# Order of the expert units: the first light one is the third, two pairs of heavy ones stand in the middle, and the first gate is made piece by piece

## The chip, the cores and the metric

One core of one Trainium2 chip runs the whole program. The time is the device time of one launch in microseconds; the median of three runs of the kernel before is 1301.4 us (1299.74 to 1305.11).

## The reference, cut to what matters

Two layers of a decoder trunk over 256 tokens of width 1024. The first layer ends in a dense SwiGLU, the second in a mixture of eight experts, of which each token uses two:

```python
def moe_swiglu(x, w_router, we_gate, we_up, we_down):      # D_FF_EXPERT = 3584
    logits = (x @ w_router).astype(jnp.float32)
    top_vals, top_idx = lax.top_k(logits, TOP_K)            # TOP_K = 2
    gates = jax.nn.softmax(top_vals, axis=-1)
    ...
    for e in range(N_EXPERTS):                              # 8
        out = out + combine[..., e:e + 1] * swiglu(x, we_gate[e], we_up[e], we_down[e])
```

All weights are float32: 3 x 1024 x 3584 numbers for each expert, 352 MB for the eight. The products are made from two rounded parts of each number (high and low), as high x high, high x low and low x high.

## The kernel before

After the router, the kernel gathers each expert's tokens and works expert by expert, each in four quarters of its 3584 columns. A quarter is a **unit**; there are 32. Four experts are **heavy** (up to 128 tokens; three matmuls for each product) and the four with the fewest tokens are **light** (up to 64 tokens, high and low part side by side in one operand; two matmuls for each product, and a fold of the two halves afterwards). `ORDER` (L80) is the order of the units by kind: `HHH`, twelve times `LH`, `H`, `LLLL`. Expert 0 is the first heavy one; which expert is any other is known only after the router, and SyncE reads that from `expert_of` before it issues the first load of a light unit (L526 to L529).

**Pieces.** The weights of a unit come as 12 pieces: 4 of the gate and 4 of the up projection (128 x 1792 numbers, 0.92 MB each), and of the down projection 3 of 1.05 MB and one of 0.52 MB, 11.0 MB in all. A piece passes five stations: SyncE loads it into one of 6 slots of `raw` (`load`, L443; it waits until the piece six places ahead has been split); ScalarE rounds it into one of 4 slots of `w_hi` (L656; it waits until TensorE has used the piece four places ahead); VectorE makes `w_lo` (`split_lo`, L1018); TensorE multiplies. A unit i multiplies 4 gate pieces, and then its up pieces mixed with the down pieces of unit i-1 as `ududduud` (`mixed`, L120). Between the first and second gate piece TensorE transposes the h of unit i-1 (`turn_h`, L2026), for which VectorE must have made it (`times_up`, L1385).

**Order on the engines.** ScalarE and VectorE go through the pieces in the same order, with other work at fixed places of unit i (loops at L904 and L1526): after the last piece of the unit comes the work on fetched tokens (`round_tokens` on ScalarE, `rest_of_tokens` on VectorE), then two pieces of the next unit, then `times_up`, `after_up` (routing tables in units 0 to 3) and the next two pieces.

**Tokens of an expert.** For all experts but 0 the tokens are fetched: TensorE sums the indices (`sum_tokens`, L2147, in the units of `SUM_AT`), VectorE copies them (`know_tokens`), GpSimd issues an indirect DMA into `more_rows` (`fetch_tokens`), TensorE transposes the rows (`turn_tokens`, L2156, in the units of `VISITS`), ScalarE and VectorE split them, and TensorE waits for both before the next unit's gate (`before_gate`). For the first light expert the sum is made in the middle of unit 1 and the transposition in the middle of unit 2, ahead of its third up piece (`amid_up`, L2188).

**The first gate** (`first_gate`, L2198) makes high x high for all 4 pieces, then high x low for all, then low x high for all, and gives up each piece in the last round.

Of the kernel before, what the change touches and what calls it, by code (L numbers as in the profile page):

```python
# [14 lines left out]
def hybrid_trunk_kernel(nc, x_in, w_in, conv_w, v_g, v_b, w_s, b_s, out_g, w_out, ln1_g, ln1_b, ln2_g, ln2_b,  # L15
# [11 lines left out]
    NT = TOK // P  # L27
# [51 lines left out]

    ORDER = "HHH" + "LH" * 12 + "H" + "L" * QUARTERS  # L80
    assert ORDER.count("H") == HEAVIES * QUARTERS and ORDER.count("L") == LIGHTS * QUARTERS

# [19 lines left out]
    FETCHED = (("L", 0), ("H", 1), ("L", 1), ("H", 2), ("L", 2), ("H", 3), LAST_ONE)  # L102
    VISITS = ((2, 0), (3, 1), (8, 2), (10, 3), (13, 4), (16, 5), (20, 6))
    KEPT = sorted([ek for ek in FETCHED if ek != LAST_ONE] + [("H", 0)], key=lambda ek: units(*ek)[-1])
    SUM_AT = (1, 4, 5, 6)
    PICK_AT = 7
# [46 lines left out]
    with ctx:  # L153
# [168 lines left out]
        gateT_bank, upT_bank = turn[:, 2, 0:PART], turn[:, 3, 0:PART]  # L322
        sums_bank = turn[:, 1, PART:PART + 4]
        tokens_bank = turn[:, 0:2, :].rearrange("p b c -> p (b c)")
# [117 lines left out]
        def _(sp):  # L442
# [81 lines left out]
            for which, i, pair in IN_ORDER:  # L524
                k, s = expert_step(i)
                if (which, i, pair) == ("gate", ORDER.index("L"), 0):  # L526
                    sp.wait_ge(tokens_known, 1)
                    ranked_expert = [sp.value_load(expert_of[0:1, q:q + 1], min_val=1, max_val=E - 1)
                                     for q in range(OTHERS)]  # L529
# [475 lines left out]
        def _(dve):  # L1005
# [413 lines left out]
            def rank_experts():  # L1419
# [16 lines left out]
                step(nc.vector.tensor_reduce(slot_at, ranked, X, ALU.add))  # L1436
                choose(0)
                step(nc.vector.tensor_tensor(below, at_rank, slot_iota[:, 1:E].unsqueeze(1).to_broadcast(
                    [P, OTHERS, OTHERS]), ALU.mult))
                step(nc.vector.tensor_reduce(expert_at, below, X, ALU.add))  # L1440
                nc.vector.tensor_copy(expert_of, expert_at)

# [52 lines left out]
            def know_tokens(j):  # L1495
                n = len(FETCHED[2 * j:2 * j + 2])
                dve.wait_ge(tokens_summed, j + 1)
                nc.vector.tensor_copy(token_of[:, 2 * j:2 * j + n],
                                      sums_bank[:, 0:2 * n:2]).then_inc(tokens_known, 1)

# [25 lines left out]
            for i in range(N_UNITS):  # L1526
# [7 lines left out]
                else:  # L1534
                    if i:
                        rest_of_h(i - 1)
                    splits(b, b + 1)
                split_lo(b + 2)
                if kept_at(i) is not None and KEPT[kept_at(i)][0] == "L":
                    fold_ys(kept_at(i))  # L1540
# [4 lines left out]
                splits(b + 3, min(unit_end, ahead))  # L1545
                if i in SUM_AT:
                    know_tokens(SUM_AT.index(i))
# [116 lines left out]
        def _(pe):  # L1664
# [482 lines left out]
            def sum_tokens(j):  # L2147

                pe.wait_ge(pick_ready, NT + j + 1)
                for c in range(len(FETCHED[2 * j:2 * j + 2])):  # L2150
                    for n in range(NT):
                        last = nc.tensor.matmul(sums_bank[:, 2 * c:2 * c + 2], pick[:, n, c, :],
                                                token_ids[:, n, :], start=(n == 0), stop=(n == NT - 1))
                last.then_inc(tokens_summed, 1)
# [24 lines left out]
            def before_gate(i):  # L2179

                if visit_at(i - 1) is not None:
                    pe.wait_ge(xg_done, visit_at(i - 1) + 1)
                if i - 1 in SUM_AT:
                    pe.wait_ge(tokens_known, SUM_AT.index(i - 1) + 1)
# [3 lines left out]
            def amid_up(i):  # L2188

                gate_left(i)  # L2190
                if i in SUM_AT:
                    sum_tokens(SUM_AT.index(i))
                if visit_at(i) is not None:
                    turn_tokens(visit_at(i))
# [3 lines left out]
            def first_gate():  # L2198

                w = [wide_rows([a[:, (MOE_AT + pair) % PARTS, :] for a in (w_hi, w_lo)]) for pair in range(4)]  # L2200
                for k in range(KD):
# [4 lines left out]
                    for c in range(2):  # L2206
                        nc.tensor.matmul(gate_banks[:, c, :], xg_hi[0][:, k, :], w[k // 2][0][:, k % 2, c, :],
                                         start=(k == 0), stop=False)
                for k in range(KD):
                    if k % 2 == 0:  # L2210
                        pe.wait_ge(*split_of(MOE_AT + k // 2))
                    for c in range(2):
                        nc.tensor.matmul(gate_banks[:, c, :], xg_hi[0][:, k, :], w[k // 2][1][:, k % 2, c, :],
                                         start=False, stop=False)
                for k in range(KD):
                    if k % 4 == 0:
                        pe.wait_ge(xg_lo_ready, k // 4 + 1)
                    for c in range(2):
                        last = nc.tensor.matmul(gate_banks[:, c, :], xg_lo[0][:, k, :], w[k // 2][0][:, k % 2, c, :],
                                                start=False, stop=(k == KD - 1))  # L2220
                    if k % 2:
                        last.then_inc(piece_used, 1)

# [26 lines left out]
            for i in range(N_UNITS):  # L2250
                if i == 0:
                    first_gate()
                else:
                    before_gate(i)
                    for pair in range(4):
                        if pair == 1:
                            turn_h(i - 1)
                        rows_pair(i, 0, pair)
                    turned_left(i - 1)
                pairs = {"u": 0, "d": 0}  # L2260
                for c in mixed(i):
# [4 lines left out]
                    else:  # L2266
                        if pairs[c] == 2 and i == N_UNITS - 1:
                            turn_h(i)
                        down(i - 1, pairs[c])
                    pairs[c] += 1  # L2270
# [57 lines left out]
```

## Time and profile before

| | before |
|---|---|
| median of 3 runs | 1301.4 us |
| the profiled execution | 1302.68 us, its span 1300.9 us |
| busy share of the span: TensorE, VectorE, ScalarE | 96%, 85%, 72% |
| granted TensorE clock, mean over the span | 0.993 |
| mean over the span of what the DMAs moved | 334 GB/s |

The expert stage runs from 374 us (first gate) to 1286 us (last down product). Its units follow each other on TensorE, and a stretch from the end of one to the end of the next can be read from the busy times by window. A line of such a view gives the stretch, its length, the busy time and instruction count of TensorE (PE), its weight loads (PEld), VectorE (DVE), ScalarE (ACT) and GpSimd (POOL), then the granted clock, the share of time that the DMA engines were busy, and the rate in GB/s. TensorE's idle time is the length less its busy time.

### The profile page before, as it was taken

To read this page: it belongs to the slowest core of one execution; us is meant where nothing else is said; L and a number is where in the kernel's file an instruction comes from. 1 tells how busy PE (TensorE), PEld (TensorE's weight loads), DVE (VectorE), ACT (ScalarE), POOL (GpSimd) and SP (SyncE) were. 2 spreads that over 40 slices of the span, in tenths; PEclk is the share of its full clock that TensorE was granted. 3 is DMA by queue.
4 is the path that set the end of the run, shared out by engine and by line. 5 is a ranking of instruction groups with operands and counts; after the bars stand their busy time and mean duration, and the time that the engine had idled before them with its cause. 6 is when DMAs were issued, how large, how long until landed. Compare 5 with 4: busy or idle time off the path is not lost.

```text
span 1300.9 us, 16398 instructions
## 1 busy us (share of the span) xinstructions
PE 1247.5 (96%) x6471; PEld 1087.2 (84%) x6471; DVE 1105.6 (85%) x871; ACT 930.2 (72%) x720; POOL 43.3 (3%) x57
## 2 busy tenths in 40 slices
PE   9999999999999999999999999999999999999884
PEld 8988888888888888888897888889888898988673
DVE  6977555577979899898989999899998989999895
ACT  5575444454867787788878788788887878888772
POOL 1100000001010000000000000000000000000010
PEclk9999999999999999999999999999999999999997
DMA  9947555536559999999999999999999999999991
GB/s 325 345 141 273 187 189 193 194 135 218 167 186 363 344 412 358 409 410 406 398 405 396 402 410 411 403 396 398 413 394 411 400 402 412 400 406 397 410 410 37
DMA packets 143558, 434.52 MB, mean 334 GB/s; under 512 B 8964, under 2 KB 50996, under 8 KB 131188
## 3 DMA queue, kind: packets, MB, share of 16 engines
q1 hardware_dynamic: 139936, 421.07, 84.6%
q0 software_dynamic: 3456, 12.32, 2.7%
q8 instruction: 53, 0.87, 0.3%
q14 instruction: 29, 0.24, 0.1%
q10 hardware_dynamic: 84, 0.02, 0.0%
HBM read 428.40 MB, written 4.98 MB: 333 GB/s over the span
## 4 chain that ended last, share of the span: by engine, by line
PE 70%; DVE 17%; DMA 6%; ACT 4%; issue 3%; POOL 0%; SPq 0%; ACTq 0%; DVEq 0%; POOLq 0%
DVE w_lo L1016 14%; PE turn L1679 7%; PE turn L1681 7%; PE turn L1680 7%; PE accp L1679 6%; PE accp L1681 6%; PE accp L1680 6%; PE turn L1791 4%; PE turn L1788 4%; ACT w_hi L656 3%; PE turn L2022 3%; DMA raw<-in_we_gate 3%; PE accp L2049 3%; PE accp L2051 3%; DMA raw<-in_we_up 2%
## 5 line engine op out<-in xcount | busy, mean ns | idle before, releaser
L1016 DVE TENSOR_TENSOR w_lo<-raw,w_hi 128x2048 fp32r<-128x2048 f32 (+3 forms) x449 | 900.4, 2041 | 113.5 <-ACT w_hi L656 110.7
L656 ACT CAST w_hi<-raw 128x1792 fp32r<-128x1792 f32 (+2 forms) x443 | 755.4, 1725 | 185.2 <-PE turn L1681 48.7
L2099 PE MATMUL turn<-w_hi,t_both 128*128 128x448 f32 x512 | 192.1, 375 | 20.5 <-DVE w_lo L1016 18.8
L2100 PE MATMUL turn<-w_lo,t_both 128*128 128x448 f32 x512 | 187.3, 366 | 0.0
L1679 PE MATMUL turn<-w_hi,a_hi 128*128 128x448 f32 x496 | 184.2, 371 | 2.9 <-DVE w_lo L1016 2.8
L1680 PE MATMUL turn<-w_lo,a_hi 128*128 128x448 f32 x496 | 181.8, 366 | 0.0
L1681 PE MATMUL turn<-w_hi,a_lo 128*128 128x448 f32 x496 | 181.7, 366 | 0.0
L2099 PEld LDWEIGHTS turn<-w_hi,t_both 128*128 128x128 f32 x512 | 96.1, 188 | 40.3 <-issue 18.4
L1679 PEld LDWEIGHTS turn<-w_hi,a_hi 128*128 128x128 f32 x496 | 93.2, 188 | 14.0 <-DVE w_lo L1016 3.7
L2100 PEld LDWEIGHTS turn<-w_lo,t_both 128*128 128x128 f32 x512 | 96.4, 188 | 7.9
L1680 PEld LDWEIGHTS turn<-w_lo,a_hi 128*128 128x128 f32 x496 | 93.2, 188 | 8.4
L1681 PEld LDWEIGHTS turn<-w_hi,a_lo 128*128 128x128 f32 x496 | 93.2, 188 | 8.1
L1679 PE MATMUL accp<-w_hi,hT_hi 128*128 128x512 f32 x224 | 89.0, 397 | 5.7 <-DVE w_lo L1016 5.7
L1788 PE MATMUL turn<-t_both,w_hi 128*128 128x512 f32 x232 | 91.8, 396 | 0.0
L1791 PE MATMUL turn<-t_both,w_hi 128*128 128x512 f32 x232 | 91.8, 396 | 0.0
L1681 PE MATMUL accp<-w_hi,hT_lo 128*128 128x512 f32 x224 | 87.5, 391 | 0.0
L1680 PE MATMUL accp<-w_lo,hT_hi 128*128 128x512 f32 x224 | 87.4, 390 | 0.0
L2049 PE MATMUL accp<-w_hi,hT_hi 128*128 128x512 f32 x210 | 83.8, 399 | 3.2 <-DVE w_lo L1016 1.9
L2051 PE MATMUL accp<-w_lo,hT_hi 128*128 128x512 f32 x210 | 82.8, 394 | 0.0
L1790 PE MATMUL turn<-t_both,w_lo 128*128 128x256 f32 x232 | 64.6, 278 | 0.0
L1789 PE MATMUL turn<-t_both,w_lo 128*128 128x256 f32 x232 | 64.3, 277 | 0.0
L1679 PE MATMUL accp<-w_hi,a_hi 128*128 128x512 f32 x152 | 59.5, 391 | 0.0
(291 smaller groups left out, 1562.0 us busy)
## 6 DMA issues: line engine op xcount, KB each, us to landing
raw<-in_we_gate SPq DMA_DIRECT2D x128, 896.0 KB, 7.6
raw<-in_we_up SPq DMA_DIRECT2D x128, 896.0 KB, 9.4
raw<-in_we_down SPq DMA_DIRECT2D x96, 1024.0 KB, 10.0
raw<-in_w_in SPq DMA_DIRECT2D x18, 1024.0 KB, 8.9
raw<-in_we_down SPq DMA_DIRECT2D x32, 512.0 KB, 7.7
raw<-in_w_down SPq DMA_DIRECT2D x11, 1024.0 KB, 5.0
raw<-in_w_gate SPq DMA_DIRECT2D x10, 1024.0 KB, 5.2
raw<-in_w_up SPq DMA_DIRECT2D x10, 1024.0 KB, 5.2
```

What stands on the lines that cost most here:

```text
L656: nc.scalar.copy(w_hi[:, p % PARTS, 0:filled(p)], raw[:, p % RING, 0:filled(p)]).then_inc(hi_done, 1)
L1016: return nc.vector.tensor_tensor(out, whole, hi.bitcast(f32), ALU.subtract)
L1679: nc.tensor.matmul(to, lh, rh, start=start, stop=False, **group)
L1680: nc.tensor.matmul(to, lh, rl, start=False, stop=False, **group)
L1681: return nc.tensor.matmul(to, ll, rh, start=False, stop=stop, **group)
L1788: nc.tensor.matmul(whole, wh[:, k, at], xT_pair[:, k, :], start=(k == 0), stop=False)
L1790: nc.tensor.matmul(first, wl[:, k + 1, at], xT_hi[:, k + 1, :], start=False, stop=False)
L1791: last = nc.tensor.matmul(whole, wh[:, k + 1, at], xT_pair[:, k + 1, :], start=False, stop=(k == KD - 2))
L2049: nc.tensor.matmul(accp[:, 2 + c, :], hT_packed[:, block, :], wh[:, j, cols], start=(first and block == 0), stop=False)
L2051: last = nc.tensor.matmul(accp[:, 2 + c, :], hT_packed[:, block, :], wl[:, j, cols], start=False, stop=(last_one and block == BLOCKS - 1))
L2099: nc.tensor.matmul(to[:, c, :], few, wh[:, kk, c, :], start=(k == 0), stop=False)
L2100: last = nc.tensor.matmul(to[:, c, :], few, wl[:, kk, c, :], start=False, stop=(k == KD - 1))
```

## The change

`ORDER` gets its first light unit at place 2 (counted from 0) in place of 3, one heavy unit stands beside another at places 9 and 10 and at 18 and 19, and only one stands ahead of the last four light units. `VISITS` and `SUM_AT` follow. The first light expert's indices are summed right after the gate of unit 1, its tokens are transposed ahead of the last down piece of unit 1 (after all up pieces), SyncE waits for the table of experts alone, and `first_gate` finishes one piece after the other.

```diff
-    ORDER = "HHH" + "LH" * 12 + "H" + "L" * QUARTERS
+    ORDER = "HH" + "LHLHLHLHH" * 2 + "LHLHLHLH" + "L" * QUARTERS
...
-    VISITS = ((2, 0), (3, 1), (8, 2), (10, 3), (13, 4), (16, 5), (20, 6))
+    VISITS = ((1, 0), (4, 1), (8, 2), (10, 3), (13, 4), (16, 5), (21, 6))
...
-    SUM_AT = (1, 4, 5, 6)
+    SUM_AT = (1, 3, 5, 6)
...
-        sums_bank = turn[:, 1, PART:PART + 4]
+        first_sums, later_sums = accp[:, 2, 0:4], turn[:, 1, PART:PART + 4]
...
-                    sp.wait_ge(tokens_known, 1)
+                    sp.wait_ge(pick_ready, NT + 1)
...
-                choose(0)
                 step(nc.vector.tensor_tensor(below, at_rank, slot_iota[:, 1:E].unsqueeze(1).to_broadcast(
                     [P, OTHERS, OTHERS]), ALU.mult))
                 step(nc.vector.tensor_reduce(expert_at, below, X, ALU.add))
-                nc.vector.tensor_copy(expert_of, expert_at)
+                step(nc.vector.tensor_copy(expert_of, expert_at))
+                choose(0)
...
                 split_lo(b + 2)
+                if i == SUM_AT[0]:
+                    know_tokens(0)
...
-                if i in SUM_AT:
+                if i in SUM_AT[1:]:
                     know_tokens(SUM_AT.index(i))
...
-                if visit_at(i) is not None:
+                if visit_at(i):
                     turn_tokens(visit_at(i))
...
-                for k in range(KD):
-                    if k % 2 == 0:
-                        pe.wait_ge(*split_of(MOE_AT + k // 2))
-                    for c in range(2):
-                        nc.tensor.matmul(gate_banks[:, c, :], xg_hi[0][:, k, :], w[k // 2][1][:, k % 2, c, :],
-                                         start=False, stop=False)
-                for k in range(KD):
-                    if k % 4 == 0:
-                        pe.wait_ge(xg_lo_ready, k // 4 + 1)
-                    for c in range(2):
-                        last = nc.tensor.matmul(gate_banks[:, c, :], xg_lo[0][:, k, :], w[k // 2][0][:, k % 2, c, :],
-                                                start=False, stop=(k == KD - 1))
-                    if k % 2:
-                        last.then_inc(piece_used, 1)
+                for pair in range(4):
+                    pe.wait_ge(*split_of(MOE_AT + pair))
+                    pe.wait_ge(xg_lo_ready, pair // 2 + 1)
+                    for k in (2 * pair, 2 * pair + 1):
+                        for c in range(2):
+                            nc.tensor.matmul(gate_banks[:, c, :], xg_hi[0][:, k, :], w[pair][1][:, k % 2, c, :],
+                                             start=False, stop=False)
+                            last = nc.tensor.matmul(gate_banks[:, c, :], xg_lo[0][:, k, :], w[pair][0][:, k % 2, c, :],
+                                                    start=False, stop=(k == KD - 1))
+                    last.then_inc(piece_used, 1)
...
+                    if i == SUM_AT[0]:
+                        sum_tokens(0)
                     turned_left(i - 1)
...
+                        if pairs[c] == 3 and visit_at(i) == 0:
+                            turn_tokens(0)
                         down(i - 1, pairs[c])
```

## Rows read from the trace of the kernel before

**Rows 1.** The page, its parts 1 and 2: TensorE over the span; GB/s in 40 slices

```profile
PE 1247.5 (96%) x6471; PEld 1087.2 (84%) x6471; DVE 1105.6 (85%) x871; ACT 930.2 (72%) x720; POOL 43.3 (3%) x57
GB/s 325 345 141 273 187 189 193 194 135 218 167 186 363 344 412 358 409 410 406 398 405 396 402 410 411 403 396 398 413 394 411 400 402 412 400 406 397 410 410 37
```

**Rows 2.** Busy times by window: later units 22 (H), 23 (L), 27 (H after H)

```profile
988.53:1017.87 29.34, 29.34 (x154) 26.56 (x153) 25.43 (x15) 23.12 (x17) 0.58 (x1) 1.00 1.01 399
1017.87:1043.22 25.35, 24.09 (x114) 20.50 (x114) 24.73 (x15) 21.73 (x16) 0.00 (x0) 1.00 1.02 412
1127.25:1157.09 29.84, 29.84 (x146) 26.73 (x146) 27.14 (x17) 23.24 (x16) 0.55 (x1) 1.00 1.02 413
```

**Rows 3.** The same view of two light units with longer waits, 11 and 19

```profile
683.53:710.39 26.86, 24.44 (x114) 20.42 (x114) 26.03 (x16) 22.55 (x16) 0.59 (x1) 1.00 1.02 394
906.82:933.01 26.19, 24.35 (x115) 20.42 (x114) 25.59 (x16) 22.18 (x16) 0.59 (x1) 1.00 1.02 413
```

**Rows 4.** The same view of the last light units 28, 30 and 31

```profile
1157.09:1181.94 24.85, 23.87 (x115) 20.58 (x114) 24.17 (x15) 21.21 (x16) 0.00 (x0) 1.00 0.99 383
1207.72:1237.79 30.07, 24.88 (x120) 19.77 (x120) 25.06 (x15) 22.59 (x17) 0.00 (x0) 1.00 1.02 410
1237.79:1271.84 34.05, 29.46 (x148) 24.18 (x148) 32.65 (x20) 25.51 (x19) 3.50 (x2) 0.95 0.92 371
```

**Rows 5.** The same view, units 0 to 6, from TensorE's end of one to the next

```profile
374.20:395.83 21.63, 20.14 (x99) 18.19 (x99) 18.34 (x20) 13.75 (x10) 0.00 (x0) 1.00 0.70 248
395.83:426.61 30.78, 30.59 (x150) 27.11 (x150) 28.03 (x31) 22.32 (x15) 0.97 (x1) 1.00 0.98 371
426.61:458.58 31.97, 31.09 (x154) 27.08 (x154) 29.10 (x42) 23.09 (x17) 0.98 (x1) 1.00 0.96 348
458.58:485.19 26.61, 25.09 (x121) 20.91 (x120) 25.25 (x20) 21.46 (x16) 0.00 (x0) 1.00 1.02 410
485.19:515.46 30.27, 30.05 (x158) 27.27 (x158) 26.93 (x22) 22.91 (x17) 2.45 (x1) 1.00 0.97 365
515.46:542.13 26.67, 25.21 (x118) 20.36 (x116) 24.90 (x19) 20.56 (x14) 0.00 (x0) 1.00 1.02 395
542.13:572.14 30.01, 29.80 (x156) 27.05 (x156) 26.96 (x19) 24.42 (x19) 0.58 (x1) 1.00 1.02 410
```

**Rows 6.** Chain of waits, first gate and token transposition: start, length, engine, tile, line

```profile
374.38 3.35 PE turn L2207 x16
377.73 3.31 PE turn L2213 x16
381.04 0.84 PE turn L2219 x4
381.96 1.70 ACT w_hi L656
...
451.49 0.64 PE turn L2161 x8
```

**Rows 7.** Timeline of GpSimd: the fetch of the first light expert's tokens

```profile
420.71 0.97 POOL L617 DMA_INDIRECT more_rows<-token_rows,numbers  x1 [50.82 <-DVE numbers L1498]
```

**Rows 8.** Timeline of ScalarE and VectorE, between units 1 and 2 and between 2 and 3

```profile
419.99 1.69 ACT L656 CAST w_hi<-raw 128x1792 fp32r<-128x1792 f32 x1 [1.67 <-PE accp L1681]
...
452.17 0.59 ACT L887 CAST t_both<-turn 128x512 fp32r<-128x512 f32 x1 [2.25 <-PE turn L2161]
...
426.55 1.08 DVE L1388 TENSOR_TENSOR h_e<-turn,y_work 128x896 f32<-128x896 f32 x1
...
431.09 3.96 DVE L1016 TENSOR_TENSOR w_lo<-raw,w_hi 128x1792 fp32r<-128x1792 f32 x2 [0.26 <-DVE ranking L1475]
434.97 1.08 DVE L1016 TENSOR_TENSOR hT_lo<-turn,hT_hi 128x896 fp32r<-128x896 f32 x1
435.97 15.56 DVE L1016 TENSOR_TENSOR w_lo<-raw,w_hi 128x1792 fp32r<-128x1792 f32 x8
```

**Rows 9.** Busy times by window: three light up pieces

```profile
461.03:466.25 5.22, 5.18 (x24) 4.01 (x23) 5.22 (x4) 5.18 (x4) 0.00 (x0) 1.00 1.02 414
```

More of the change, by code:

```diff
@@ L1498, in know_tokens @@
                 nc.vector.tensor_copy(token_of[:, 2 * j:2 * j + n],
-                                      sums_bank[:, 0:2 * n:2]).then_inc(tokens_known, 1)
+                                      (later_sums if j else first_sums)[:, 0:2 * n:2]).then_inc(tokens_known, 1)
             def add_rows(j):
@@ L2151, in sum_tokens @@
                     for n in range(NT):
-                        last = nc.tensor.matmul(sums_bank[:, 2 * c:2 * c + 2], pick[:, n, c, :],
+                        last = nc.tensor.matmul((later_sums if j else first_sums)[:, 2 * c:2 * c + 2], pick[:, n, c, :],
                                                 token_ids[:, n, :], start=(n == 0), stop=(n == NT - 1))
@@ L2182, in before_gate @@
                     pe.wait_ge(xg_done, visit_at(i - 1) + 1)
-                if i - 1 in SUM_AT:
+                if i - 1 in SUM_AT[1:]:
                     pe.wait_ge(tokens_known, SUM_AT.index(i - 1) + 1)
@@ L2190, in amid_up @@
                 gate_left(i)
-                if i in SUM_AT:
+                if i in SUM_AT[1:]:
                     sum_tokens(SUM_AT.index(i))
-                if visit_at(i) is not None:
+                if visit_at(i):
                     turn_tokens(visit_at(i))
```

## Prediction, written before the changed kernel ran

> **What bounds the kernel now.** I read the page first: TensorE is busy 96% of the span, and from the 15th slice on the DMAs move about 400 GB/s [rows 1]. Two resources are near their limit, so the averages don't decide. Next I cut the expert stage at the ends of its units on TensorE. Three paces come out: a heavy unit after a light one takes 29.34 us without a hole, a heavy one after a heavy one 29.84, a light one after a heavy one 25.35 with 1.26 idle [rows 2]. The light unit's hole is VectorE's: it makes 12 pieces and two passes on h in a unit in which TensorE needs only 24.1 us. The transfers need 11.01 MB at the 412 GB/s of the best windows = 26.7 us a unit, 53.4 a pair against 54.7. So in the middle TensorE, with VectorE's hole once a pair, sets the pace, and the transfers are 1.3 us a pair faster; where GpSimd's transfers take part of the DMA time, the hole in the light unit grows (2.42 and 1.84 us; four such units, 11, 15, 17 and 19, by 2.4 us in all over 1.26) [rows 3]. The last four light units are bound by the transfers: unit 30 takes 30.07 us, of which TensorE works 24.88 [rows 4]. The early units are above the pace: unit 1 30.78 (pace 29.84), unit 2 31.97 (29.84), unit 3 26.61 (25.35), unit 4 30.27 (29.34), unit 5 26.67 (25.35), unit 6 30.01 (29.34) [rows 2, 5]. That is what a change of order can win: the sum of the pace over the 32 units is the same for both orders, since each has three heavy units behind a heavy one and twelve light ones behind a heavy one.
>
> **The change, part by part.** I count TensorE's idle and extra time up to the end of the last heavy unit, and then pass it to the end.
>
> First gate. Before, piece 0 is given up after 36 matmuls; the chain shows 16 in 3.35, 16 in 3.31, 4 in 0.84, then ScalarE's cast of the fifth piece at 381.96 [rows 6]. After, it takes 16 + 8 matmuls: 374.4 + 3.35 + 1.67 = 379.4, so the cast and VectorE's split come 2.4 us earlier. TensorE itself ends the 48 products at the same 384.3, and only its wait of 1.49 us (21.63 - 20.14) goes [rows 5]: **-1.5**. Nothing else is late next: the fifth piece is then split by 383.5.
>
> Tables and SyncE. `choose(0)` comes about 0.7 us later on VectorE; its reader is now the sum after the gate of unit 1, some 5 us later: 0. SyncE reads the experts' numbers ahead of piece 0 of unit 2, which is not wanted on ScalarE until about 424: 0. The first fetch is issued earlier: `know_tokens(0)` moves ahead of five splits (about 409 in place of 420). In the trace GpSimd issued it at 420.71 [rows 7], 31 us before its transposition, so its landing time can't be read as a need; the transposition is now at about 423.7, 14 us after the issue. A piece of 0.92 MB at 412 GB/s takes 2.2 us; I take it as landed, and if the fetch were slower than 14 us all that follows moves by the difference.
>
> The transposition for unit 2. This is the costly part. Before, it stands ahead of two up pieces and a down piece, about 6.4 us of TensorE's work; ScalarE stood 2.25 us waiting for it at 452.17 [rows 8] and TensorE felt nothing. After, it stands behind both up pieces, with one down piece of 6 matmuls (1.4 us) as cover, while ScalarE and VectorE still have to pass it before they may touch the gate pieces of unit 2. Queued behind ScalarE's wait are all four casts of that gate, queued behind VectorE's are the four splits, `times_up(1)` and the routing tables. With unit 1 about 1.5 us early: last up piece done 423.7; transposed 424.4 (0.64 [rows 6]); down piece done 425.8; ScalarE tokens 425.0 (0.59), cast 426.7 (1.70); VectorE split 428.7 (1.98, half of 3.96 [rows 8]). TensorE stands from 425.8 to 428.7: hole 2.9. A light pair of pieces is 8 matmuls, 1.65 (24 in 5.18 [rows 9]; the same for gate). Second split 430.7, h product (1.08) 431.7: hole 1.3 before the transposition of h, which ends 432.6. Before, VectorE needed from 427.6 to 431.1 for the tables and another 3.96 for two splits [rows 8]; after, 431.7 to 435.2, splits at 437.2 and 439.1. TensorE had finished the second piece at 434.3: hole 2.9; third piece 438.8: hole 0.3; then h's low part and the first up piece (442.1): hole 1.3, and 0.6 at the first down piece. VectorE goes on without a gap as it did at 435.97 (8 in 15.56 us), ends its unit near 455.5 against 451.5, and TensorE is full again. Holes 9.3 in place of the paced 1.26: **+8.0**; the token transposition now counts in unit 1: +0.7; unit 2's own excess before goes (31.97 - 29.84): **-2.1**. From the two sides: 0 if pieces already split cover the wait, 9.3 if nothing does; the dependence of each station on the one before leaves at most the 1.4 us of the down piece as cover, so I take 8.0.
>
> Units 3 to 6. Heavy unit 3 has the sum of indices and a late start (0.8 over pace, before 1.3): -0.5. Light unit 4 enters with TensorE full, but VectorE's choice and weights fall between its second and third gate piece, and it carries a heavy token transposition: +2.4 over pace against 0.9: +1.5. Units 5 and 6: 0.5 and 0.4 against 1.3 and 0.7: **-1.1** [rows 5].
>
> Sum to here: -1.5 + 8.0 + 0.7 - 2.1 - 0.5 + 1.5 - 1.1 = **+5.0**.
>
> The middle. A TensorE that runs 5 us later no longer feels the extra holes of the four light units: **-2.4** [rows 3]. The two pairs of heavy units cost 29.84 in place of 29.34 each, as the pairs that go did: 0. So the last heavy unit ends 2.6 later.
>
> The last four light units go by the transfers. Before, the lag of a pair of heavies at their head slows these (383 in place of 412 GB/s in 24.85 us = 1.7 us of transfer time [rows 4]); with one heavy there, this goes: -1.7. The write of light expert 2's rows (0.26 MB, 0.6 us) moves into this stretch: +0.6. In all **+1.5 us**: the profiled execution's 1302.68 becomes 1304.2. It is 1.3 above the median, so I predict 1302.9, say 1303 for the median.
>
> The holes near 428 and 436 are 2.9 us each; the longest that a row of an early unit can hold is 1.49, and the granted clock stays at 1.00 in all of them [rows 5], while it is 0.95 in 1237.79 to 1271.84, with 4.59 us idle [rows 4]. The Trainium skill (TensorE: Matmul & The Clock Gate, Part 1) has an idle TensorE fall back to half its clock. By that rule one such fall would cost what the last row shows, 5% of 34 us = 1.7, and the sum would be +3.2; by the rows of the early units it is 0.
>
> **The rivals.** (A) *The early stretch was the loss and goes.* If splits made ahead cover the wait, unit 2 keeps its pace: the +1.5 above becomes 1.5 - 8.0 = -6.5, 1296.2 for the profiled execution and 1295 for the median. For it: transfers in units 1 and 2 run at 371 and 348 GB/s. Against it: ScalarE already waited 2.25 us with far more cover. The Trainium skill (Perfetto Trace Analysis, Optimization Strategy) advises interleaving regimes whose most-contended engine differs, which is this case.
>
> (B) *The transfers are the true line from unit 5 on.* Then the hole of 8 us is won back, and only their own lead counts: the first gate frees pieces 2.4 us earlier, unit 3's heavy work takes it back in part: -1, 1300.4. For it: 410 GB/s in units 3 and 6 [rows 5]. Against: the 1.3 us a pair.
>
> (C) *The pairs of heavy units in the middle stop the transfers.* At units 9/10 and 18/19 TensorE enters 5 us late; each heavy pair puts it 2 x 29.6 - 2 x 26.7 = 5.8 us further behind. From the point where its lag is more than the four split pieces and the filled slots hold, a load waits, and units 11 and 20 then wait for data. I price each at 3.1 (29.84 - 26.7): +1.5 + 2 x 3.1 = +7.7, 1309. For it: transfers lost 1.7 behind the old pair. Against: one such pair at pace ran with 413 GB/s [rows 2].
>
> **Chances.** Forecast 0.46 (1299 to 1307), A 0.17, B 0.18, C 0.17, others 0.02. One measurement of this kernel tells no less than about 0.5%, 6.5 us, from no change; so faster by over 0.5% is 0.16 (most of A), within it 0.65 (forecast, B, the rest), slower 0.19 (C and a hole larger than 9.3). The range that should hold 8 of 10 takes in the ends of A and C: 1294.5 to 1310.5.
>
> **What would show it.** Right: TensorE idle some 9 us between 425 and 445; ScalarE waiting over 6 us for the token transposition between units 1 and 2; VectorE idle as long; the fifth piece's cast near 379.5; two heavies in a row at 29.8; the last heavy unit ending near 1160 (before 1157.1). Wrong: a unit 2 of 26 us (A), a last heavy ending at or before 1156 (B), units 11 or 20 longer than 27 us with waits on DMA (C), or a fetch that lands after 423.7.

## The result, and the profile after the change

| | before | after |
|---|---|---|
| median | 1300.91 us, 20 runs (1298.43 to 1305.11) | 1304.2 us, 20 runs (1302.78 to 1307.81) |
| ratio to before, 95% interval | 1 | 1.0028, 1.002 to 1.0035 |
| profiled execution, its span | 1302.68, 1300.9 us | 1306.46, 1304.7 us |
| last heavy unit ends on TensorE | 1157.09 | 1159.84 |
| first three quarters of the last down product's columns end ("end") | 1285.71 | 1289.39 |

In every kernel here the last quarter of those columns ends 3.33 to 3.34 us after "end" (1289.05 before, 1292.73 after), so differences of "end" are differences of the last product too.

The change costs 3.6 us by the ratio (1300.91 x 0.0028); the two medians are 3.3 apart. The forecast was 1303.0, with a sum of +1.5 where the ratio shows +3.6 and the two profiled executions +3.8. Both lie inside 0.5%.

The share of time in which TensorE is busy is 96%, as before [rows 1]. Of the GB/s in the expert stage the 12th to 16th slices differ most (208, 338, 336, 387, 380 for 186, 363, 344, 412, 358). The page after, parts 1 and 2:

```profile
span 1304.7 us, 16401 instructions
...
GB/s 320 343 145 268 188 192 192 193 135 216 171 208 338 336 387 380 399 409 398 406 407 391 388 411 411 403 386 404 411 397 400 403 400 399 413 398 412 410 413 41
```

Cut at the ends of the units, as in [rows 5] (stretch, length, then busy time and count of PE, PEld, DVE, ACT, POOL, the granted clock, DMA share, GB/s). Units 0 to 6 after the change:

```profile
374.87:394.91 20.04, 20.04 (x99) 18.23 (x99) 18.69 (x20) 14.00 (x10) 0.00 (x0) 1.00 0.81 291
394.91:426.33 31.42, 31.42 (x158) 27.27 (x156) 24.44 (x29) 19.28 (x14) 3.56 (x2) 1.00 0.91 337
426.33:459.14 32.81, 27.35 (x114) 22.36 (x115) 31.11 (x41) 25.90 (x19) 0.18 (x1) 0.90 0.92 337
459.14:488.94 29.80, 29.80 (x158) 27.00 (x157) 26.02 (x20) 22.20 (x16) 0.00 (x0) 1.00 1.00 384
488.94:516.86 27.92, 25.48 (x122) 20.84 (x120) 26.56 (x25) 22.09 (x16) 0.91 (x1) 1.00 1.00 389
516.86:547.16 30.30, 30.08 (x158) 27.28 (x158) 26.25 (x17) 23.03 (x17) 0.00 (x0) 1.00 1.02 380
547.16:573.11 25.95, 24.49 (x116) 20.65 (x116) 25.32 (x18) 21.85 (x16) 0.00 (x0) 1.00 1.02 412
```

The first gate has no idle time any more (20.04 of 20.04). Unit 2, a light one with 24.1 us of work at pace [rows 2], takes 32.81 us: TensorE idles 5.46, and its own 114 matmuls take 27.35 because the granted clock is 0.90. How it comes to stand there is on ScalarE, VectorE and GpSimd, the counterparts of [rows 7, 8] (start, length, engine, line, operation; in brackets the idle time before it and its releaser):

```profile
380.13 3.36 ACT L656 CAST w_hi<-raw 128x1792 fp32r<-128x1792 f32 x2 [2.11 <-PE turn L2218]
...
424.80 0.59 ACT L887 CAST t_both<-turn 128x512 fp32r<-128x512 f32 x1 [7.11 <-PE turn L2163]
```

```profile
425.42 0.69 DVE L1016 TENSOR_TENSOR t_both<-turn,t_both 128x512 fp32r<-128x512 f32 x1 [6.45 <-ACT t_both L887]
427.00 3.96 DVE L1016 TENSOR_TENSOR w_lo<-raw,w_hi 128x1792 fp32r<-128x1792 f32 x2 [0.90 <-ACT w_hi L656]
430.88 1.08 DVE L1388 TENSOR_TENSOR h_e<-turn,y_work 128x896 f32<-128x896 f32 x1
431.88 0.87 DVE L1125 TENSOR_SCALAR pick<-slot_iota,ranking 128x128 fp32r<-128x128 f32 x4
...
435.19 3.96 DVE L1016 TENSOR_TENSOR w_lo<-raw,w_hi 128x1792 fp32r<-128x1792 f32 x2
```

```profile
409.84 2.76 POOL L617 DMA_INDIRECT more_rows<-token_rows,numbers  x1 [39.30 <-DVE numbers L1498]
```

ScalarE stands 7.11 us until the transposition, VectorE 6.45; then VectorE does two splits, the h product, 3.3 us of routing tables (431.88 to 435.19) and only then the next two splits. TensorE waits for each of them. Its waits in unit 2 (line, what it waited for: us in total, times, longest):

```profile
PE turn L2101 <- DVE w_lo L1016: 4.5, 3, 2.8
PE turn L2017 <- DVE h_e L1388: 0.6, 1, 0.6
PE accp L1681 <- DVE w_lo L1016: 0.3, 1, 0.3
```

The clock, which the forecast held at 1.00, falls. The windows around the first hole:

```profile
426.30:429.20 2.90, 0.05 (x2) 0.06 (x1) 2.20 (x2) 2.90 (x3) 0.21 (x1) 1.00 1.01 416
429.20:431.00 1.80, 1.80 (x8) 1.48 (x8) 1.80 (x2) 1.80 (x2) 0.00 (x0) 0.86 1.02 327
431.00:433.00 2.00, 1.38 (x7) 0.98 (x6) 2.00 (x11) 0.73 (x1) 0.00 (x0) 0.50 1.02 400
433.00:435.00 2.00, 2.00 (x8) 1.87 (x7) 1.73 (x15) 1.17 (x2) 0.00 (x0) 0.50 1.04 355
435.00:437.00 2.00, 1.78 (x5) 1.03 (x4) 1.97 (x2) 1.45 (x2) 0.00 (x0) 0.50 0.47 197
437.00:439.00 2.00, 1.73 (x8) 1.44 (x8) 2.00 (x2) 1.78 (x1) 0.00 (x0) 0.92 0.38 66
```

TensorE works 0.05 us in a stretch of 2.90; behind it the clock is 0.86 and then 0.50 (1.2 of 2.4 GHz), and it is back within 437 to 439. In the same place the transfers fall to 66 GB/s: the slots are full, and SyncE waits up to 5.9 us for a split before it may load again (between 430 and 442).

The heavy pair in the middle (units 9, 10, 11), the last heavy unit and the last light ones:

```profile
628.82:658.16 29.34, 29.34 (x154) 26.56 (x153) 25.80 (x15) 22.46 (x16) 0.00 (x0) 1.00 1.02 402
658.16:688.88 30.72, 30.72 (x154) 27.57 (x154) 27.85 (x17) 24.06 (x17) 1.51 (x2) 1.00 1.03 408
688.88:714.11 25.23, 23.95 (x114) 20.50 (x114) 24.54 (x15) 21.48 (x16) 0.00 (x0) 1.00 1.00 388
1130.50:1159.84 29.34, 29.34 (x153) 26.55 (x153) 26.28 (x15) 23.25 (x17) 0.00 (x0) 1.00 1.02 395
1159.84:1186.05 26.21, 24.38 (x115) 20.42 (x114) 25.76 (x16) 22.98 (x17) 0.55 (x1) 1.00 1.02 414
1186.05:1211.84 25.79, 24.11 (x121) 19.74 (x119) 23.49 (x14) 21.09 (x16) 4.95 (x3) 1.00 1.02 412
1211.84:1241.78 29.94, 24.86 (x121) 19.77 (x120) 25.13 (x15) 22.64 (x17) 0.00 (x0) 1.00 1.02 410
1241.78:1275.65 33.87, 29.34 (x149) 24.34 (x148) 32.63 (x20) 25.54 (x19) 3.49 (x2) 0.95 0.93 377
```

Heavy units in a row lose nothing: 30.72 with no idle time, 0.9 over the 29.84 of [rows 2] with 8 more matmuls (the transposition of tokens), and the light unit behind keeps 25.23. Unit 28, the first of the last four, takes 26.21 where it took 24.85 [rows 4].

### The profile page after: what moved, and what is told of

Its sections match the earlier page's. It is cut to its first block, busy times and chain, and to the rows that moved or that the text cites. A ratio compares the mean times of both kernels' runs of the same rounds, so it can differ in the third digit from the quotient of the medians.

```text
span 1304.7 us, 16401 instructions
## 1 busy us (share of the span) xinstructions
PE 1249.5 (96%) x6471; PEld 1089.2 (83%) x6471; DVE 1104.5 (85%) x871; ACT 931.5 (71%) x720; POOL 43.1 (3%) x57
## 4 chain that ended last, share of the span: by engine, by line
PE 74%; DVE 16%; DMA 4%; ACT 3%; issue 2%; SPq 0%; ACTq 0%; DVEq 0%
DVE w_lo L1016 12%; PE turn L1681 8%; PE turn L1683 8%; PE turn L1682 8%; PE accp L1681 6%; PE accp L1682 6%; PE accp L1683 6%; PE turn L1793 4%; PE turn L1790 4%; PE turn L2024 3%; ACT w_hi L656 3%; PE accp L2051 3%; PE accp L2053 3%; PE turn L2101 2%; PE turn L2102 2%
```

## The experiments

Every kernel was timed beside the kernel before on the same chip. "Unit 2", "u27" and "end" are of the profiled execution: the length of unit 2 on TensorE, the end of the last heavy unit, and the row of that name in the table above.

**a1: the first gate alone.** The new `first_gate` in the kernel before.

```diff
+ for pair in range(4):
+     pe.wait_ge(*split_of(MOE_AT + pair))
+     ...                       # the three products of this piece, then the piece is given up
- ...                           # before: high x high of all pieces, high x low of all, low x high of all
```

> The kernel before with the new first gate alone. Theory (TensorE's wait of 1.49 us at the first up piece goes, and TensorE sets the pace until the last four units): the cast of the fifth piece comes 2.3 us earlier, the wait is 0, and the end comes up to 1.5 us earlier, 1299.4 to 1300.9 against 1300.9, ratio 0.9988 to 1.0. Rival (the transfers are the line from unit 5 on): the early gain shows in units 0 to 2 and is gone at the end, ratio 1.000.

Measured: 1299.3 us (1296.66 to 1303.36, 11 runs), ratio 0.9988 [0.9978, 0.9998]; u27 1155.62, end 1283.72. The window of unit 0, whose first product begins at 374.76 here:

```profile
374.76:394.80 20.04, 20.04 (x99) 18.23 (x99) 18.69 (x20) 14.01 (x10) 0.00 (x0) 1.00 0.81 288
```

No idle time: 20.04 us in place of 21.63. The last heavy unit ends 1.47 us earlier than in the kernel before. So the 1.6 us of the first gate is gained, and nothing behind gives it back. The changed kernel is some 5.2 us behind this one (0.9988 to 1.0028).

**a2: the transposition earlier.** The changed kernel, with the transposition of the first fetched tokens ahead of the third up piece of unit 1, two up pieces earlier.

```diff
-                if visit_at(i):
+                if visit_at(i) is not None:
                     turn_tokens(visit_at(i))
...
-                        if pairs[c] == 3 and visit_at(i) == 0:
-                            turn_tokens(0)
```

> The changed kernel with one edit: the first light expert's tokens are transposed ahead of the third up piece of unit 1, as all others are, and not ahead of its last down piece. Theory (the late transposition holds ScalarE and VectorE, and so TensorE's unit 2): ScalarE's wait for it falls from 7.1 us to under 3, TensorE's holes in unit 2 from 5.5 us plus 3.3 us of slow matmuls to 3 or less (the tables remain), unit 2 takes 28 to 29 us in place of 32.8, and the end comes 2 to 4 us earlier than the changed kernel, 1300 to 1302, ratio 0.9995 to 1.001. Rival 1 (the fetch has not landed at 419): TensorE waits for it inside unit 1 and nothing is won, ratio 1.003. Rival 2 (the pairs of heavy units cost the 3 us): unit 2 gets short and the end stays, ratio 1.003.

Measured: 1300.05 us (1298.78 to 1300.7, 11 runs), ratio 0.9994 [0.9985, 1.0002]. ScalarE's wait and unit 2:

```profile
419.14 0.59 ACT L887 CAST t_both<-turn 128x512 fp32r<-128x512 f32 x1 [2.25 <-PE turn L2163]
```

```profile
425.56:453.72 28.16, 24.35 (x114) 20.42 (x114) 27.17 (x40) 22.69 (x17) 0.00 (x0) 1.00 0.99 383
```

The wait is the 2.25 us of [rows 8]. The hole ahead of unit 2 is gone and the clock stays at 1.00; unit 2 is 4.65 us shorter, and the time falls by 4.4 us (0.0034 x 1300.9). What is left is 3.8 us of idle time, of which 3.4 are waits for splits behind the tables.

**a3: the tables into the wait.** The changed kernel, late transposition kept; VectorE makes the routing tables of the second half-round (`choose(1)`, `usable_choices()`) while it waits for that transposition, not between two splits of unit 2.

```diff
+                if i == 1:
+                    choose(1)
+                    usable_choices()
                 if visit_at(i) is not None:
                     rest_of_tokens(visit_at(i))
...
-                if i in SUM_AT:
+                if i in SUM_AT[1:]:
                     ...choose
-                if i == 1:
-                    usable_choices()
```

> The changed kernel with one edit: the routing tables that VectorE makes in unit 1 after the h product (3.3 us) stand ahead of its work on the fetched tokens, in the 6.5 us in which it waits for them. Theory: the hole between the second and third gate piece of unit 2 goes, VectorE's unit 2 ends 3.3 us earlier, unit 2 takes about 29.5 us in place of 32.8, and the end comes 2 to 3 us earlier than the changed kernel, 1301 to 1302, ratio 1.000 to 1.0015. Rival (the transfers, not unit 2, set the later part): the end moves by under 1 us, ratio 1.002 to 1.003.

Measured: 1301.38 us (1300.0 to 1302.7, 11 runs), ratio 1.0005 [0.9996, 1.0014]. Unit 2:

```profile
425.84:455.34 29.50, 25.68 (x115) 21.98 (x115) 28.19 (x16) 25.46 (x19) 0.18 (x1) 0.94 1.01 374
```

3.3 us less than in the changed kernel, as many as the tables take; the hole ahead of the unit stays (longest wait 2.9), and with it a fall of the clock to 0.50, for 3.4 us here.

**a4: no fall of the clock.** The changed kernel with 12 unused matmuls of 512 columns behind the last down piece of unit 1, where TensorE has nothing to do. The added products are written where nothing reads them.

```diff
                         down(i - 1, pairs[c])
+                        if pairs[c] == 3 and i == 1:
+                            for _ in range(12):
+                                nc.tensor.matmul(accp[:, 3, :], a_hi[:, 0:P], a_hi[:, 0:BANK], start=True, stop=True)
```

> The changed kernel with 12 idle matmuls of 512 columns (about 2.6 us) added after the last down piece of unit 1; their result is not used. They fill TensorE's hole of 2.85 us, after which the granted clock was 0.50 for some 7 us. Theory: the clock stays at 1.00, but the slow matmuls had lain in waits for VectorE, so unit 2 gets shorter by under 0.7 us and the ratio stays at 1.002 to 1.003. Rival (the fall of the clock is the loss): unit 2 gets shorter by the 3.3 us of extra busy time and the ratio falls to 1.0005 or less.

Measured: 1304.5 us (1303.7 to 1308.41, 6 runs), ratio 1.0036 [1.0024, 1.0049]. The windows of the old hole and of the stretch behind it, and unit 2:

```profile
425.60:428.40 2.80, 2.66 (x13) 1.92 (x11) 2.20 (x2) 2.80 (x3) 0.09 (x1) 1.00 1.02 420
...
432.00:436.00 4.00, 1.94 (x11) 1.47 (x10) 3.69 (x19) 3.65 (x3) 0.00 (x0) 1.00 0.80 296
...
425.51:458.32 32.81, 27.67 (x127) 22.52 (x126) 31.11 (x41) 25.79 (x19) 0.18 (x1) 1.00 0.91 333
```

The clock is full in all of it, and unit 2 takes the same 32.81 us. The slow matmuls of the changed kernel lie in time in which TensorE would wait for VectorE anyway (1.94 us busy of 4.00 here): the fall costs nothing that can be measured.

**b1: one pair into the middle, in the kernel before.** Of the pair ahead of the last four light units, one heavy unit goes to places 10 and 11.

```diff
-    ORDER = "HHH" + "LH" * 12 + "H" + "L" * QUARTERS
+    ORDER = "HHH" + "LHLHLHLHH" + "LH" * 8 + "L" * QUARTERS
```

> The kernel before with one edit: one heavy unit of the pair that stands ahead of the last four light units is moved to the middle (a pair at units 10 and 11, the last heavy unit follows a light one). The start, the first gate and the third unit are untouched. My theory: a pair in the middle costs TensorE nothing (in the changed kernel units 9 to 11 and 18 to 20 kept the pace of 29.3 to 29.8 and 25.2 us), and what the move costs is the stock of landed pieces for the last four light units: at the end of unit 27 the landed data were 11.80 us ahead of TensorE in the kernel before and 8.97 us in the changed one. So the end comes 0.5 to 1.2 us later, ratio 1.0004 to 1.001. Rival C of the prediction, that pairs in the middle stop the transfers: 3 us or more, ratio 1.0025 or over, with idle time of TensorE in units 11 to 14. Third theory, that the order is worth nothing anywhere: ratio 0.9997 to 1.0003 and the same 11.80 us ahead.

**b2: one pair back, in the changed kernel.**

```diff
-    ORDER = "HH" + "LHLHLHLHH" * 2 + "LHLHLHLH" + "L" * QUARTERS
+    ORDER = "HH" + "LHLHLHLHH" + "LH" * 8 + "H" + "L" * QUARTERS
```

> The changed kernel with one edit: the second of its middle pairs is taken out and its extra heavy unit stands ahead of the last four light units, as in the kernel before. First light unit still third, first gate still by pieces, one pair in the middle. My theory: the landed data are again some 11.8 us ahead of TensorE at the end of unit 27, the last four light units take 0.5 to 1.2 us less than in the changed kernel, and the time is 1303.0 to 1303.7 us, ratio to the kernel before 1.0016 to 1.0022 beside 1.0028. If the last stretch is bound by something else than the stock, nothing changes: 1.0028. If the middle pair kept back transfers, it gains more than 1.5 us.

Measured: b1 1300.54 us (1299.37 to 1302.15, 11 runs), ratio 1.0000 [0.9991, 1.0009]; b2 1304.32 us (1303.33 to 1305.97, 8 runs), ratio 1.0029 [1.0019, 1.004], beside 1.0028 without the edit. I had expected a loss of 0.5 to 1.2 us in b1 and a gain of as much in b2, from the stock of landed pieces; neither shows. In the medians the place of a pair is worth nothing within about 1.2 us, either way. In b1 the middle pair and the first of the last four, which now follows a single heavy unit:

```profile
683.32:713.16 29.84, 29.84 (x146) 26.75 (x146) 27.53 (x17) 23.30 (x16) 0.59 (x1) 1.00 1.02 394
...
1155.26:1181.43 26.17, 24.35 (x115) 20.42 (x114) 25.75 (x16) 22.75 (x17) 0.55 (x1) 1.00 1.02 414
```

and the same unit of b2, behind a pair again:

```profile
1159.69:1184.58 24.89, 23.88 (x115) 20.58 (x114) 24.18 (x15) 21.22 (x16) 0.00 (x0) 1.00 0.99 390
```

The pair in the middle runs at 29.84. Unit 28 takes 26.2 without a pair ahead of it and 24.9 with one, in both kernels.

**b3: everything that helps, in the changed kernel**: a2's and a3's edits, and b2's order.

> The changed kernel with three edits: the token transposition stands ahead of the third up piece of unit 1, the routing tables of the second half-round are made by VectorE while it waits for that transposition, and the pair stands ahead of the last four light units. My theory: the hole at the start of unit 2 goes (as when the transposition alone was moved) and the 3.8 us that were left in unit 2 shrink, since VectorE no longer makes the tables between hT_hi and hT_lo: unit 2 takes 26 to 27.5 us, and the end comes at 1297.5 to 1299.5 us, ratio 0.9975 to 0.999. If the transfers are the line by then (rival B's mechanism, the landings of the later units), TensorE's gain in unit 2 comes back as idle time in the light units 8 to 26 and the time is that of the early transposition alone, 1300, ratio 0.9994.

Measured: 1297.15 us (1295.76 to 1299.49, 11 runs), ratio 0.9978 [0.9969, 0.9987], end 1279.95. Unit 2:

```profile
425.98:452.31 26.33, 24.34 (x115) 20.42 (x114) 24.73 (x15) 22.44 (x17) 0.00 (x0) 1.00 1.02 410
```

The light unit in third place keeps nearly its pace (26.33, idle 1.99), 6.5 us less than in the changed kernel; the median is 6.5 us lower as well (0.0050 x 1300.9). What TensorE wins at 452 us arrives at the end.

**b4: the same care for the old order.** The kernel before with the new first gate, and with `usable_choices()` moved into VectorE's wait for the transposition in unit 2.

```diff
-                if i == 1:
-                    usable_choices()
...
+                if i == 2:
+                    usable_choices()
                 if visit_at(i) is not None:
                     rest_of_tokens(visit_at(i))
```

> The kernel before, in its old order of units, with the first gate by pieces and with the routing choices of the second half-round made by VectorE in its wait for the token transposition. My theory: the idle 0.9 us at TensorE in unit 2 goes beside the 1.5 us of the first gate: 1298.3 to 1298.9 us, ratio 0.998 to 0.9985. Rival: the 0.9 us is not set by the choices and the ratio is that of the first gate alone, 0.9988.

Measured: 1296.88 us (1296.33 to 1299.2, 7 runs), ratio 0.9973 [0.9962, 0.9985]. Unit 2, a heavy one here:

```profile
425.09:455.80 30.71, 30.71 (x155) 27.25 (x154) 28.85 (x41) 23.10 (x17) 0.98 (x1) 1.00 0.97 375
```

The 0.88 us of idle time of [rows 5] is gone, and the unit 1.2 us shorter than in a1 (31.93). So the old order, handled with the same care, is as fast as the new one. I had expected 0.998 to 0.9985, and the median is lower than that; of the 2 us below a1 by the ratios, unit 2 explains 1.2.

**c1 and c2: the place of the pairs, with b3's other edits.** c1 has no pair in the middle and three heavy units ahead of the last four light ones; c2 has the changed kernel's order.

```diff
-    ORDER = "HH" + "LHLHLHLHH" + "LH" * 8 + "H" + "L" * QUARTERS     # b3
+    ORDER = "HH" + "LH" * 12 + "HH" + "L" * QUARTERS                 # c1
+    ORDER = "HH" + "LHLHLHLHH" * 2 + "LHLHLHLH" + "L" * QUARTERS     # c2
```

> The kernel of b3 (early transposition, tables in the wait) with no pair in the middle: three heavy units in a row stand ahead of the last four light ones. Stock theory: TensorE falls further behind the landed data in each heavy unit behind another, so at the end of unit 27 they are 12 us or more ahead of it (b3: 10.22; without a pair 9.0 to 9.6), the last stretch takes 126 us or less (b3 126.92, without a pair 128.7 to 129.6), and what this gains is paid back by the middle, which keeps its extra holes in light units: within 1 us of b3, ratio 0.997 to 0.9985. Rival, that the last stretch is set by its transfers alone and the differences between the kernels are scatter: 127 to 129 us whatever stands ahead. Third, that three heavy units stop the transfers: lead 12 us but a landing rate under 390 GB/s in units 25 to 28, end 1 us or more later than b3.

> The kernel of b3 with the pairs where the changed kernel has them, both in the middle and none ahead of the last four light units: early transposition and tables in the wait, together. If the place of the pairs is worth nothing in the median (as b1 and b2 say, 1.0000 and 1.0029 beside 1.0028), the ratio is that of b3, 0.9975 to 0.998, though the last stretch takes 128.7 to 129.6 us in place of 126.9 and the lead at the end of unit 27 is 9.0 to 9.6. If the stock decides, it is 1 us slower than b3: 0.9985 to 0.999.

Measured: c1 1299.32 us (1297.93 to 1301.08, 12 runs), ratio 0.9984 [0.9976, 0.9993]; c2 1298.46 us (1296.6 to 1299.29, 9 runs), ratio 0.9977 [0.9967, 0.9988]. c2 equals b3. In c1 the third heavy unit in a row:

```profile
1125.45:1155.33 29.88, 29.88 (x147) 26.76 (x146) 25.69 (x16) 21.79 (x15) 0.00 (x0) 1.00 1.00 375
```

The transfers fall to 375 GB/s, where the second in a row still had 413 [rows 2]. For these kernels I worked out, from the landing of each piece's last packet, when the pieces of unit 27 had all landed:

```
        landed   TensorE   ahead   end       TensorE to end   pair ahead of the last four
before  1145.30  1157.09   11.80   1285.71   128.62           yes
after   1150.87  1159.84    8.97   1289.39   129.55           no
a1      1144.91  1155.62   10.70   1283.72   128.10           yes
a2      1145.01  1154.02    9.01   1283.24   129.22           no
b1      1146.25  1155.26    9.01   1284.45   129.19           no
b2      1149.25  1159.69   10.44   1286.82   127.13           yes
b3      1142.81  1153.03   10.22   1279.95   126.92           yes
b4      1144.01  1154.38   10.37   1282.20   127.82           yes
c2      1142.19  1151.46    9.27   1279.56   128.10           no
c1      1142.36  1155.33   12.97   1283.24   127.91           three
```

With a pair the last stretch takes 126.9 to 128.6, without one 128.1 to 129.6, and the stock of landed pieces is larger with one. But c1, with the largest stock, isn't shorter still: my stock theory said 126 or less. Its third heavy unit ran with a slower transfer, as the third theory had it. And c2, without the pair, is as fast as b3 in the median. So the stock of landed pieces isn't what sets the end; the difference in the last stretch is largely unit 28's 1.3 us, of which unit 27 gives back 0.5. And most of what c1's "end" lies behind b3's (3.3 us) is there before the last stretch: 2.3 us at the end of unit 27. Where they come from stands in the next section.

## Why the prediction was right, and where its sum was off

The forecast (slightly slower, inside 0.5%) held, and so did the mechanism of its largest term, unit 2. Two terms did not: the middle came out at its number for another reason, and the last four light units went the other way. Its steps, against the profiled executions:

| step | predicted | measured |
|---|---|---|
| first gate | -1.5 | -1.6 in the profiled pair, -1.6 in a1 |
| start of the first gate (no step) | 0 | +0.67 |
| unit 1, the transposition in it | +0.7 | 31.42 - 30.78 = +0.6 |
| unit 2 (holes +8.0, old excess -2.1) | +5.9 | (32.81 - 25.35) - (31.97 - 29.84) = +5.3 |
| unit 3 | -0.5 | (29.80 - 29.34) - (26.61 - 25.35) = -0.8 |
| unit 4 | +1.5 | (27.92 - 25.35) - (30.27 - 29.34) = +1.6 |
| units 5 and 6 | -1.1 | (0.96 + 0.60) - (1.32 + 0.67) = -0.4 |
| middle, to the end of unit 27 | -2.4 | (1159.84 - 1157.09) less the rows above = -2.7 |
| last four light units | -1.1 | 129.55 - 128.62 = +0.9 |
| sum | +1.5 | +3.7 |

**Unit 2, station by station.** The last down piece of unit 1 ended at 426.33 (forecast 425.8), TensorE stood 2.85 us there (2.9); the tables ended at 435.16 (435.2); ScalarE waited 7.11 us (over 6). The fetch landed 7.8 us after its issue at 409.84, well before the 424.1 at which TensorE needed it, so my taking it as landed was right. I had asked for some 9 us of idle time between 425 and 445; there are 5.47, because 3.3 us of what I had down as waiting went into matmuls at half the clock. a2 and a3 show the two parts one at a time: the place of the transposition is worth 4.4 us of the median, the tables between the splits 3.0 (1.0028 to 1.0005).

**The clock.** I held it at 1.00 by rows in which no hole was longer than 1.49 us, and it fell. The Trainium skill's rule (TensorE: Matmul & The Clock Gate, Part 1) had it right that an idle TensorE falls back to half its clock; here it did so behind a hole of 2.85 us. The cost that I attached to the rule, 1.7 us, isn't there: a4 keeps the clock full and gains nothing. My zero for the term was right for another reason than I gave: behind the hole VectorE sets the pace, and TensorE has time to be slow in.

**The step that missed most is "the last four light units go by the transfers": -1.7 and +0.6, measured +0.9.** I read the 383 GB/s of unit 28 [rows 4] as a loss that the heavy pair causes, and so as a gain when the pair goes. Without a pair the rate in unit 28 is 414, as I said, but the unit is longer: 26.21 with 1.83 idle against 24.85 with 0.98. VectorE shows why. In the kernel before it has five splits in a row at this place; in the changed kernel the finished rows of the light expert whose last unit stands two places ahead are added here:

```profile
1162.91 10.56 DVE L1016 TENSOR_TENSOR w_lo<-raw,w_hi 128x1792 fp32r<-128x1792 f32 x5
```

```profile
1166.13 6.15 DVE L1016 TENSOR_TENSOR w_lo<-raw,w_hi 128x1792 fp32r<-128x1792 f32 x3
1172.20 1.21 DVE L1413 TENSOR_TENSOR ys_rows<-accp,ys_rows 64x1024 f32<-64x1024 f32 x1
1173.33 4.47 DVE L1016 TENSOR_TENSOR w_lo<-raw,w_hi 128x2048 fp32r<-128x2048 f32 x2
```

Behind a heavy pair this addition falls into the second heavy unit, where VectorE has time to spare; behind a single one it falls into a light unit, where VectorE is the bound. My ledger gave the light units behind a single heavy one 25.35 everywhere. From unit 28's end to "end" the changed kernel takes 103.34 us and the kernel before 103.77 (1285.71 - 1181.94): 0.4 less, where I gave the transfers 1.1. Over the twelve kernels this stretch takes 101.9 to 103.8 us, so these two single executions don't show that they win anything. Unit 28 alone is +1.36.

**The middle: the right number for the wrong reason.** I let the extra holes of the middle go because TensorE would run 5 us later. In the five kernels with the changed order it reaches the end of unit 6 at 573.11 (after), 572.27 (a4), 569.27 (a3), 567.67 (a2) and 565.85 (c2), and from there to the end of unit 27 it takes 586.73, 585.73, 586.89, 586.35 and 585.61 us: an arrival 7 us earlier brings nothing back. Units 15 and 17, two of the four whose holes were to go, kept them (0.98 us above the pace together before, 1.47 after). What differs is again where the additions fall. There is one for each of the first three light experts. In the kernel before the first stands in light unit 11 and the second in light unit 19, which are the two long ones of [rows 3]; in the changed kernel they stand in the heavy units 10 and 19. The first one, before and after:

```profile
696.23 1.21 DVE L1413 TENSOR_TENSOR ys_rows<-accp,ys_rows 64x1024 f32<-64x1024 f32 x1
```

```profile
670.51 1.21 DVE L1413 TENSOR_TENSOR ys_rows<-accp,ys_rows 64x1024 f32<-64x1024 f32 x1
```

Over all twelve profiled executions, the time of units 7 to 27 above the paces of [rows 2]:

| additions in light units, of units 7 to 27 | kernels | above the paces, us |
|---|---|---|
| two | before, a1, b4, c1 | 8.2 to 8.8 |
| one | b1, b2, b3 | 5.6 to 6.7 |
| none | after, a2, a3, a4, c2 | 4.4 to 5.7 |

Every light unit behind a single heavy one that holds an addition takes 0.8 to 1.7 us over 25.35; what is left in the last row stands in other units and has other causes. So the two pairs in the middle win 2.7 us there, and the missing pair at the end costs 1.4 in unit 28. This also says why b1, b2 and c2 showed nothing: none of them changes how many additions fall in light units in the whole stage (two in before and b1, one in after, b2, b3 and c2); c1 goes from b3's one to two, and its "end" is 3.3 us later, though its median is only 0.8 us behind by the ratios, with overlapping intervals. All this is read from the traces, and no run moved an addition by itself: ScalarE's copy ahead of it (1.0 us) and GpSimd's write of the rows behind it move with it.

Of the 2.2 us between sum and profiled difference, 0.67 is the scatter of single executions: the first gate began that much later (374.09 to 374.87 over the twelve; b2 and a4, with the same code up to there as the changed kernel, at 374.26 and 374.10).

**The rivals.** A, that the early stretch is won, asked for splits made ahead over the wait; the wait was there, and unit 2 took 32.81 and not 26. With the transposition early and the tables in the wait it does take 26.3 to 26.4 (b3, c2): the order would have allowed that part of A, and two placements prevented it. A's price of 1295 is not reached even so (1297.15 in b3). B, that the transfers win the hole back, is refuted: b3 and c2 recover 6.5 us in unit 2 and all of it stays at the end. C, that pairs in the middle stop the transfers, is refuted by b1 and by the windows of units 9 to 11; it takes a third heavy unit in a row (c1, 375 GB/s) before the rate gives way within a heavy unit.

Best measured are b4 (0.9973) and b3 (0.9978), with overlapping intervals: some 3 us below the kernel before. The order itself is worth nothing that their medians can tell; what helped was the first gate by pieces and VectorE's small work put into its waits.

## What to carry to other kernels

When a transposition or another step that two engines must pass moves behind more of TensorE's work, count all that is queued behind it on those engines: it was the largest term here, and going through the stations in order gave its first hole as 2.9 us for the 2.85 measured. Put an engine's small work into a wait that it has anyway, ahead of the waiting instruction and not behind it; that gave 3.0 us in one place and 1.2 us of a unit in another. A window with a lower transfer rate isn't a loss as long as the engine that it feeds doesn't wait: before crediting its end, see what the bound engine of the next unit takes over from the order that goes. Small work at a fixed distance behind a unit moves when the order moves: list where each piece of it lands, and let it land in units whose bound engine is another.

## What the runs showed of the hardware

A single hole of 2.85 us in a TensorE that was otherwise full brought the granted clock to 0.50 from 431 to 437 us; a matmul of 448 columns took 0.57 us there in place of 0.37. In a3 the same hole brought 0.50 for 3.4 us. Holes of 1.49 us [rows 5], of 2.3 in a2 and of 2.5 in a4 (at 434) left it at 1.00. Near the end of the stage, where TensorE has other holes too, one of 2.5 us was followed by a fall in the kernel before (0.50 from 1260 us) and not in b3, so no length of a single hole can be read off as the limit. That such a fall can be free, as in a4, was the surprise. GpSimd's first two fetches landed 7.8 and 7.1 us after their issue in the changed kernel; the first three in the kernel before took 8.1 to 10.0.
